# Expert tiles cut into two 64-row halves that stand side by side in TensorE's columns, with a new expert order

## The chip, the cores and the metric

The kernel runs on one core of a Trainium2 chip. The metric is the time of one execution on the device in microseconds (us); three runs were timed, and one further execution was taken by the profiler. The core's engines are TensorE (PE in the profile; its weight loads are listed apart as PEld), VectorE (DVE), ScalarE (ACT), GpSimd (POOL) and SyncE (SP). They run their own instruction lists and meet at semaphores. SP and POOL issue the transfers between device memory and the on-chip memory.

## The reference

The whole program is one step of a decoder layer for 1,024 prompt tokens and 32 sample tokens: a mixer, cross-attention and a mixture of experts, with a LayerNorm after each. Only the mixture of experts is touched. All 1,056 tokens (`TOK`) go through it together; each goes to the two best experts of its best group of four.

```python
N_EXPERTS = 16; N_GROUPS = 4; EXPERTS_PER_GROUP = 4; TOP_K = 2; D_EXPERT = 256; D_MODEL = 1024
...
def moe_ffn(h, w_router, router_bias, wg, wu, wd):
    x = h.reshape(b * t, d)
    s = jax.nn.sigmoid((x @ w_router).astype(jnp.float32))
    sel = (s + router_bias.astype(jnp.float32)).reshape(-1, N_GROUPS, EXPERTS_PER_GROUP)
    group_score = jnp.sum(lax.top_k(sel, TOP_K)[0], axis=-1)
    gidx = jnp.argmax(group_score, axis=-1)
    in_group = jnp.take_along_axis(sel, gidx[:, None, None], axis=1)[:, 0]
    _, local = lax.top_k(in_group, TOP_K)
    eidx = gidx[:, None] * EXPERTS_PER_GROUP + local
    ...
    hg = jnp.einsum('nd,edf->nef', x, wg)
    hu = jnp.einsum('nd,edf->nef', x, wu)
    act = jax.nn.silu(hg) * hu * combine[:, :, None].astype(x.dtype)
    y = jnp.einsum('nef,efd->nd', act, wd)
```

With the reference's inputs the 16 experts get, in order of number, 103, 113, 113, 121, 121, 168, 127, 112, 134, 161, 158, 115, 131, 151, 129 and 155 rows, 2,112 in all. These counts follow from the routing above.

## The kernel before

**Routing.** `stage_route` makes the router's products, ranks the experts of each token, and gives every (token, expert) pair a row in a list that is sorted by expert. Each expert's rows are padded to whole tiles of 128. The program is fixed before the routing is known, so it runs `MOE_TILES` = 32 tiles, the most that any routing needs. With this routing 24 are filled, and the last 8 hold no rows; they are computed all the same, with the weights of the last expert. The results are tables: the expert of each tile (`tile_expert`), the first tile after each expert (`expert_end`), and the token, gate and destination of each row.

**The expert stage.** `stage_experts` walks over the tiles. POOL gathers the 128 token rows of a tile (`gather`), and at the end adds the 128 result rows to device memory (`add_rows`, one at a time). For each tile, PE turns the rows (8 transposes, `turn_x`), multiplies by the gate and up weights (`gate_up`, 8 matmuls over 512 columns, in two parts of four), turns the hidden rows (`turn_hid`, 2 transposes) and multiplies by the down weights (`product_down`, 4 matmuls over 512 columns). In fp32 each of these matmuls is two passes, so two records in the profile. ACT and DVE take the results out of PSUM. The weights are the moving operand, and the token rows the stationary one.

One step of PE for tile t holds the first part of `gate_up(t)`, then `turn_hid(t-1)`, the second part of `gate_up(t)`, `turn_x(t+1)` and `product_down(t-1)`:

```python
                gate_up(j, u, 0, e)
                if not first:
                    turn_hid(*prev)
                gate_up(j, u, 1, e)
                if not last:
                    turn_x(*((j, u + 1) if u < U - 1 else (j + 1, 0)))
                if not first:
                    product_down(*prev, prev_e & 3)
```

ACT's step is `turned_hid(t-1)`, `silu(t)`, `turned_x(t+1)`, `finish(t-1)`; DVE's is `hidden(t)`, `turned_x(t+1)`, `finish(t-1)`. The loop is unrolled by `U` = 4.

**Weights.** An expert has 3 MB of weights, loaded by `load_expert` as three transfers of 1 MB into one of four slots (`c.xw`). The first three experts are loaded during the routing. In the expert stage SP takes the experts in turn: it waits until expert e has landed, tells PE (`w_ok`), waits until the tiles of expert e-2 are done, and issues expert e+2 into the slot that expert e-2 held.

Of the kernel before, what the change touches and what calls it, by code (L numbers as in the profile page):

```python
# [15 lines left out]
I32 = mybir.dt.int32  # L16
# [26 lines left out]
DE = 256  # L43
MOE_TILES = (2 * TOK - NE) // P + NE
ALPHA = float(2 ** 0.25)
# [59 lines left out]


def route_blocks():
# [4 lines left out]
    c = {  # L112
        "tie": row(np.arange(4)[None, :] < np.arange(4)[:, None]),
        "iota128": row(np.arange(P)),
        "iota32": row(np.arange(MOE_TILES)),
        "thr9": row(P * np.arange(9)),
        "tri16": row(np.arange(NE)[None, :] < np.arange(NE)[:, None]),
        "token": np.where(token < TOK, token - TOK, 0),
        "lane": p,
        "valid": token < TOK,  # L120
    }
    return {k: np.asarray(v, np.float32) for k, v in c.items()}
# [39 lines left out]
def setup(nc, ctx, T, O):  # L162
# [87 lines left out]
    c.row_token = ctx.enter_context(nc.sbuf_tensor("row_token", [P, MOE_TILES], I32))  # L250
    c.tile_expert = ctx.enter_context(nc.sbuf_tensor("tile_expert", [1, MOE_TILES], I32))
    c.expert_end = ctx.enter_context(nc.sbuf_tensor("expert_end", [1, NE], I32))
# [2447 lines left out]
def load_expert(c, sp, e):  # L2700

    EW = KC * DE
    for q, name in enumerate(('ex_wg', 'ex_wu', 'ex_wd')):
        sp.dma_start(c.xw[:, e % 4, q * EW:(q + 1) * EW], c.T[name][0, e].rearrange("(p k) f -> p (k f)", p=P))\
            .then_inc(c.xw_in[e % 4], 16)


def stage_route(c):
# [11 lines left out]
            rank=TE, mask=TE, mask0=TE, masked=TE, pre=TE, gs=TILES * G4, grank=TILES * G4, den=TILES,  # L2720
            tiles_cmp=NE * 9, tiles_of=NE, base_cmp=NE * NE, base=NE, ends=NE, exp_cmp=MOE_TILES * NE, exp_f=MOE_TILES,
            rk=2 * TILES, bs=2 * TILES, flo_cmp=2 * TILES * NT, flo=2 * TILES, lo=2 * TILES, hi=2 * TILES,
            slot_f=MOE_TILES, empty=MOE_TILES, one_lo=2 * TILES * P, one_hi=2 * TILES * MOE_TILES,
# [16 lines left out]
    with nc.Block() as block:  # L2740
# [49 lines left out]
        def _(dve):  # L2790
# [55 lines left out]
            for q, m in enumerate((mask0, mask1)):  # L2846
# [18 lines left out]
            ec = c.A("exp_cmp").rearrange("p (s e) -> p s e", e=NE)  # L2865
            link(vt.tensor_tensor(ec, tab("iota32", MOE_TILES).unsqueeze(2).to_broadcast([P, MOE_TILES, NE]),
                                  ends.unsqueeze(1).to_broadcast([P, MOE_TILES, NE]), ALU.is_ge))
            exp_f = c.A("exp_f")
# [3 lines left out]

            link(vt.tensor_scalar(ends, ends, 1.0, None, ALU.add))
            link(vt.tensor_copy(c.expert_end[:], ends[0:1, :]))


            rk, bs, flo, lo, hi = c.A("rk"), c.A("bs"), c.A("flo"), c.A("lo"), c.A("hi")
# [6 lines left out]
            fc = c.A("flo_cmp").rearrange("p (n j) -> p n j", j=NT)  # L2884
            link(vt.tensor_tensor(fc, rk.unsqueeze(2).to_broadcast([P, N2, NT]),
                                  tab("thr9", 9)[:, 1:9].unsqueeze(1).to_broadcast([P, N2, NT]), ALU.is_ge))
            link(vt.tensor_reduce(flo, fc, AX, ALU.add))
            link(vt.scalar_tensor_tensor(lo, flo, -float(P), rk, ALU.mult, ALU.add))
            link(vt.tensor_tensor(hi, bs, flo, ALU.add))
            link(vt.tensor_tensor(one_lo, lo.unsqueeze(2).to_broadcast([P, N2, P]),  # L2890
                                  tab("iota128", P).unsqueeze(1).to_broadcast([P, N2, P]), ALU.is_equal))
            link(vt.tensor_tensor(one_hi, hi.unsqueeze(2).to_broadcast([P, N2, MOE_TILES]),
                                  tab("iota32", MOE_TILES).unsqueeze(1).to_broadcast([P, N2, MOE_TILES]), ALU.is_equal))
            link(vt.tensor_tensor(one_gate, one_hi, c.gate.unsqueeze(2).to_broadcast([P, N2, MOE_TILES]), ALU.mult))
# [18 lines left out]
def stage_experts(c):  # L2913
# [23 lines left out]
    y_ok = [s(f"yok{q}") for q in range(2)]  # L2937
    x_turned, up, sig, hid_ok, hid_turned, hidT_ok, down = (
        s("xturned"), s("up"), s("sig"), s("hid"), s("hturned"), s("hidT"), s("down"))
    U = 4  # L2940
    J = MOE_TILES // U
    XT, UPB, HT, DNB = (0, 1), (2, 3), 4, (6, 7)

    with nc.Block() as block:
        @block.sync
        def _(sp):
            sp.sem_inc(y_ok[1], 1)
            for e in range(NE):
                sp.wait_ge(c.xw_in[e % 4], 48 * (e // 4 + 1))
                sp.sem_inc(w_ok, 1)  # L2950
                if e == 0:
                    load_expert(c, sp, 3)
                if e >= 2 and e + 2 < NE:

# [31 lines left out]
        def _(pe):  # L2986
            def expert(t):
                return pe.value_load(c.tile_expert[0:1, bass.ds(t, 1)], min_val=0, max_val=NE - 1)

            def turn_x(j, u):  # L2990

                t = j * U + u
                pe.wait_ge(x_in[u % 2], 16 * (j * 2 + u // 2 + 1))
                for q in range(2):
                    if not (isinstance(j, int) and t < 1):
                        pe.wait_ge(xT_ok[q], t)
                    for k in range(4):
                        last = nc.tensor.transpose(ps[XT[q]][:, k * P:(k + 1) * P], x[:, u % 2, slice(4 * q + k, D, KC)],
                                                   K("ident"))
                    last.then_inc(x_turned, 1)  # L3000

            def gate_up(j, u, half, e):
                t = j * U + u
                if half == 0:
# [20 lines left out]
            def product_down(j, u, slot):  # L3025
                t = j * U + u
                pe.wait_ge(hidT_ok, t + 1)
                for q in range(2):
                    if not (isinstance(j, int) and t < 1):
                        pe.wait_ge(y_ok[q], t + q)  # L3030
                    for f in range(2):
                        last = nc.tensor.matmul(ps[DNB[q]][:, :], hidT[:, u % 2, f, :], down_of[:, bass.ds(slot, 1), f, q * 512:(q + 1) * 512].rearrange("p a n -> p (a n)"),  # L3032
                                                start=(f == 0), stop=(f == 1))
                    last.then_inc(down, 1)

            def step(j, u, first, last):

                prev = (j, u - 1) if u else (j - 1, U - 1)
                e = expert(j * U + u)
                prev_e = None if first else expert(j * U + u - 1)  # L3040
                gate_up(j, u, 0, e)
# [16 lines left out]
            turn_hid(J - 1, U - 1)  # L3058
            product_down(J - 1, U - 1, expert(MOE_TILES - 1) & 3)

        @block.scalar
        def _(act):
# [15 lines left out]
            def finish(t, u, first):  # L3078

                act.wait_ge(down, 2 * t + 1)  # L3080
                if not first:
# [12 lines left out]

            turned_x(0, 0)
            for u in range(U):
                step(0, u, True, False)
# [9 lines left out]
        def _(dve):  # L3107
# [9 lines left out]
            def finish(t, u, first):  # L3117
                dve.wait_ge(down, 2 * t + 2)
# [4 lines left out]
            def step(j, u, first, last):  # L3123
                hidden(j * U + u, u)
                if not (last and u == U - 1):
# [3 lines left out]

            turned_x(0, 0)  # L3130
            for u in range(U):
                step(0, u, True, False)
# [137 lines left out]
```

## Time and profile before

| what | value |
|---|---|
| median of three runs | 1704.71 us (1702.11 to 1705.04) |
| the profiled execution's time | 1703.08 us |
| its span, first to last instruction | 1701.3 us |
| mean granted TensorE clock | 0.928 of full speed |
| PE busy / DVE busy / ACT busy | 1481.7 / 618.1 / 499.7 us |

The profile's own time is 1.8 us above its span. An engine's busy time is the union of its instructions, and a matmul's end is modelled, so the steps below are read from the starts of instructions. The expert stage runs from about 1258 us to 1657 us of the span, after the routing and before the last LayerNorm.

### The profile page before, as it was taken

To read this page: it belongs to the slowest core of one execution; us is meant where nothing else is said; L and a number is where in the kernel's file an instruction comes from. 1 tells how busy PE (TensorE), PEld (TensorE's weight loads), DVE (VectorE), ACT (ScalarE), POOL (GpSimd) and SP (SyncE) were. 2 spreads that over 40 slices of the span, in tenths; PEclk is the share of its full clock that TensorE was granted. 3 is DMA by queue.
4 is the path that set the end of the run, shared out by engine and by line. 5 is a ranking of instruction groups with operands and counts; after the bars stand their busy time and mean duration, and the time that the engine had idled before them with its cause. 6 is when DMAs were issued, how large, how long until landed. Compare 5 with 4: busy or idle time off the path is not lost. (4 is left out here: it accounts for less than half of the span.)

```text
span 1701.3 us, 24683 instructions
## 1 busy us (share of the span) xinstructions
PE 1481.7 (87%) x9721; PEld 1062.2 (62%) x9722; DVE 618.1 (36%) x1005; ACT 499.7 (29%) x1050; POOL 190.0 (11%) x176
## 2 busy tenths in 40 slices
PE   4998999689999898889979989899459999999950
PEld 2445999545597677768869877687244544544420
DVE  3323462377512234447641033575421111111107
ACT  1124133278614434441222144312001111111114
POOL 0000000023200232200000000000001221222114
PEclk9998999789979799999989999999759999999985
DMA  8110121150013400012141164432625997843435
GB/s 311 56 56 20 44 55 38 36 174 26 1 50 102 136 15 2 3 56 109 44 136 38 50 255 167 147 106 87 247 111 189 329 313 238 252 89 85 97 51 227
DMA packets 85984, 193.37 MB, mean 114 GB/s; under 512 B 13204, under 2 KB 49179, under 8 KB 79475
## 3 DMA queue, kind: packets, MB, share of 16 engines
q1 hardware_dynamic: 76523, 157.14, 25.9%
q0 software_dynamic: 9216, 33.56, 8.5%
q8 instruction: 73, 1.20, 0.3%
q10 hardware_dynamic: 144, 1.25, 0.2%
q14 instruction: 28, 0.23, 0.0%
HBM read 148.50 MB, written 43.51 MB: 113 GB/s over the span
## 5 line engine op out<-in xcount | busy, mean ns | idle before, releaser
L3012 PE MATMUL bank<-arena,hT 128*128 x512 | 233.3, 599 | 2.2 <-DVE hT L3115 2.2
L3012 PEld LDWEIGHTS bank<-arena,hT 128*128 128x128 f32 x512 | 96.1, 193 | 111.3 <-issue 111.3
L3032 PE MATMUL bank<-arena,hT 128*128 x256 | 115.3, 593 | 0.7 <-ACT hT L3070 0.7
L473 PE MATMUL bank<-arena,hT 128*128 128x512 f32 x256 | 112.8, 599 | 0.0
L3110 DVE SCALAR_TENSOR_TENSOR hT<-bank,small,hT 128x256 f32<-128x256 f32 x32 | 15.5, 484 | 224.8 <-ACT hT L3076 224.8
L2134 PE MATMUL bank<-hT_rest,f_w_high 128*128 128x352 f32 x288 | 93.4, 324 | 0.0
L473 PEld LDWEIGHTS bank<-arena,hT 128*128 128x128 f32 x256 | 48.7, 193 | 58.3 <-issue 58.3
L2972 POOL DMA_INDIRECT expert_sums<-hT,row_slot x32 | 50.7, 1586 | 276.4 <-DVE hT L3121 173.0
L3032 PEld LDWEIGHTS bank<-arena,hT 128*128 128x128 f32 x256 | 46.3, 191 | 47.2 <-issue 47.2
L2963 POOL DMA_INDIRECT hT<-tokens,row_token x32 | 31.5, 984 | 317.5 <-POOLq L2740 288.3
L2133 PE MATMUL bank<-hT_high,q_w_high 128*128 128x352 f32 x192 | 62.4, 325 | 4.0 <-DVE q_w_low L2426 4.0
L2133 PE MATMUL bank<-f_h_high_a,f_w_high 128*128 128x352 f32 x180 | 59.0, 328 | 6.7 <-DVE f_w_low L683 6.7
L2135 PE MATMUL bank<-hT_high,q_w_low 128*128 128x352 f32 x192 | 62.9, 328 | 0.0
L2134 PE MATMUL bank<-hT_low,q_w_high 128*128 128x352 f32 x192 | 62.7, 326 | 0.0
L1132 PE MATMUL bank<-arena 128*128 128x256 f32 x256 | 61.7, 401 | 0.3 <-ACT arena L1264 0.3
L2135 PE MATMUL bank<-f_h_high_a,f_w_low 128*128 128x352 f32 x180 | 58.5, 325 | 0.0
L1132 PEld LDWEIGHTS bank<-arena 128*128 128x128 f32 x256 | 51.4, 203 | 9.3 <-issue 0.6
L3070 ACT COPY hT<-bank 128x256 f32<-128x256 f32 x32 | 11.9, 372 | 148.1 <-PE bank L3022 148.1
L2134 PEld LDWEIGHTS bank<-hT_rest,f_w_high 128*128 128x128 f32 x288 | 54.9, 191 | 0.0
L3121 DVE COPY hT<-bank 128x512 f32<-128x512 f32 x32 | 22.1, 691 | 89.6 <-PE bank L3032 86.8
L2133 PE MATMUL bank<-w_w_high,w_s_high 128*128 128x512 f32 x128 | 50.5, 395 | 0.3 <-DVE w_w_low L2320 0.3
L2133 PE MATMUL bank<-o_w_high,o_s_high 128*128 128x512 f32 x128 | 50.5, 395 | 0.0
(470 smaller groups left out, 2963.7 us busy)
## 6 DMA issues: line engine op xcount, KB each, us to landing
arena<-in_ex_wg_dram SPq DMA_DIRECT2D x16, 1024.0 KB, 5.1
arena<-in_ex_wu_dram SPq DMA_DIRECT2D x16, 1024.0 KB, 8.9
arena<-in_ex_wd_dram SPq DMA_DIRECT2D x16, 1024.0 KB, 12.7
tokens<-h SPq DMA_DIRECT2D x24, 512.0 KB, 2.6
arena<-in_cache_mem_k_dram SPq DMA_DIRECT2D x8, 1024.0 KB, 4.9
arena<-in_w_in_dram SPq DMA_DIRECT2D x12, 512.0 KB, 4.1
h<-tokens SPq DMA_DIRECT2D x6, 1024.0 KB, 6.7
h<-in_x_prompt_dram SPq DMA_DIRECT2D x8, 512.0 KB, 8.8
```

The costliest lines, as they stand in the source:

```text
L473: last = nc.tensor.matmul(ps[bank][0:r, 0:n], hT[:, k, i * P:i * P + r], wt[:, k, col:col + n], start=(k == 0), stop=(k == KC - 1))
L1132: last = c.nc.tensor.matmul(c.ps[bank][:, 0:256], c.memT[:, k, m * P:(m + 1) * P], c.mw[:, n % 3, k, :], start=(k == 0), stop=(k == KC - 1))
L2133: nc.tensor.matmul(out, high, w_high, start=start, stop=False)
L2134: nc.tensor.matmul(out, high, w_low, start=False, stop=False)
L2135: return nc.tensor.matmul(out, low, w_high, start=False, stop=stop)
L2963: gp.indirect_dma_start(x[:, t % 2, :], None, c.tokens_dram, bass.IndirectOffsetOnAxis(ap=c.row_token[:, t:t + 1], axis=0)).then_inc(x_in[ ...
L2972: gp.indirect_dma_start(c.sums_dram, bass.IndirectOffsetOnAxis(ap=c.row_slot[:, t:t + 1], axis=0), y[:, t % 2, :], None, compute_op=ALU.ad ...
L3012: last = nc.tensor.matmul(ps[UPB[u % 2]][:, :], xT[:, u % 2, k, :], gate_up_of[:, bass.ds(slot, 1), :, k, :].rearrange("p a g f -> p (a g) ...
L3032: last = nc.tensor.matmul(ps[DNB[q]][:, :], hidT[:, u % 2, f, :], down_of[:, bass.ds(slot, 1), f, q * 512:(q + 1) * 512].rearrange("p a n ...
L3070: nc.scalar.copy(hidT[:, u % 2], ps[HT][:, 0:DE].rearrange("p (f t) -> p f t", f=2)).then_inc(hidT_ok, 1)
L3110: nc.vector.scalar_tensor_tensor(hid[:, u % 2, :], ps[UPB[u % 2]][:, DE:2 * DE], c.row_gate[:, bass.ds(t, 1)], sg[:, u % 2, :], ALU.mult, ...
L3121: nc.vector.tensor_copy(y[:, u % 2, 512:D], ps[DNB[1]][:, :]).then_inc(y_ok[1], 1)
```

## The change

A tile still has 128 rows, but it is now two halves of 64 (`HT_ROWS`), and each half has an expert of its own. Experts are padded to halves of 64, at least one for each expert. The program therefore has at most 48 halves, which make `MOE_TILES` = 24 tiles. With the routing above the halves of the experts in the new order are 2, 2, 3, 3, 2, 3, 3, 3, 2, 2, 3, 3, 2, 2, 2, 3, in all 40: tiles 0 to 19 are filled and 20 to 23 empty.

Each matmul of `gate_up` and `product_down` becomes two, with 64 stationary columns each: the lower half's rows against its expert's slot, written to PSUM partitions 0 to 63, and the upper half's rows against a copy of its expert's weights, written to partitions 64 to 127 of the same bank. The copies alternate between two places (`wb` in the arena, and the free `h`). ACT copies one half of the columns and DVE the other (`copy_gate_up` for tile t+1 and `copy_down` for tile t, both at the front of step t). Experts are taken in the order 0, 4, 8, 12, 1, 5, ... (`ORDER`), so that neighbours are of different groups and no token stands twice in a tile. SP loads expert e (by place in that order) when expert e-4 is done and expert e-1 has landed.

```diff
+HT_ROWS = 64
+HALVES = (2 * TOK - NE) // HT_ROWS + NE
+MOE_TILES = (HALVES + 1) // 2
...
+ORDER = [4 * (j % 4) + j // 4 for j in range(NE)]
...
+            link(vt.tensor_tensor(ec, tab("iota128", H).unsqueeze(2).to_broadcast([P, H, NE]),
+                                  ends.unsqueeze(1).to_broadcast([P, H, NE]), ALU.is_ge))
...
+    c.place(start=4 * 3 * EW, wb=3 * EW)
+    copies = [c.A("wb"), h.rearrange("p i d -> p (i d)")[:, 0:3 * EW]]
...
+    def copy_gate_up(eng, copy, t, u, z, first):
+
+        e = eng.value_load(c.tile_expert[0:1, bass.ds(2 * t + 1, 1)], min_val=0, max_val=NE - 1)
+        eng.wait_ge(w_ok, e + 1)
+        if not first:
+            eng.wait_ge(up, t - 1)
+        copy(whole[u % 2][:, 0:2, z, :], slots[:, bass.ds(e & 3, 1), 0:2, z, :].rearrange("p a q n -> p (a q) n")).then_inc(gu_ok[z], 1)
+
+    def copy_down(eng, copy, t, u, z, first):
+
+        e = eng.value_load(c.tile_expert[0:1, bass.ds(2 * t + 1, 1)], min_val=0, max_val=NE - 1)
+        eng.wait_ge(w_ok, e + 1)
+        if not first:
+            eng.wait_ge(down[1], t - 1)
+        copy(whole[u % 2][:, 2, z, :], slots[:, bass.ds(e & 3, 1), 2, z, :].rearrange("p a n -> p (a n)")).then_inc(dn_ok[z], 1)
...
             sp.sem_inc(y_ok[1], 1)
+            load_expert(c, sp, 3)
             for e in range(NE):
+                if e >= 4:
+                    sp.wait_ge(down[1], sp.value_load(c.expert_end[0:1, ORDER[e - 4]:ORDER[e - 4] + 1], min_val=1, max_val=MOE_TILES))
+                    load_expert(c, sp, e)
                 sp.wait_ge(c.xw_in[e % 4], 48 * (e // 4 + 1))
                 sp.sem_inc(w_ok, 1)
-                if e == 0:
-                    load_expert(c, sp, 3)
-                if e >= 2 and e + 2 < NE:
-
-                    sp.wait_ge(y_ok[1], sp.value_load(c.expert_end[0:1, e - 2:e - 1], min_val=1, max_val=MOE_TILES + 1))
-                    load_expert(c, sp, e + 2)
...
+                if half == 0:
+                    for q in range(2):
+                        pe.wait_ge(gu_ok[q], t + 1)
                 slot = e & 3
                 for k in range(4 * half, 4 * half + 4):
-                    last = nc.tensor.matmul(ps[UPB[u % 2]][:, :], xT[:, u % 2, k, :], gate_up_of[:, bass.ds(slot, 1), :, k, :].rearrange("p a g f -> p (a g) f"), start=(k == 0), stop=(k == KC - 1))
+                    nc.tensor.matmul(ps[UPB[u % 2]][rows_of(0), :], xT[:, u % 2, k, rows_of(0)],
+                                     gate_up_of[:, bass.ds(slot, 1), :, k, :].rearrange("p a g f -> p (a g) f"),
+                                     start=(k == 0), stop=(k == KC - 1))
+                    last = nc.tensor.matmul(ps[UPB[u % 2]][rows_of(1), :], xT[:, u % 2, k, rows_of(1)], gate_up_b[u % 2][:, :, k, :],
+                                            start=(k == 0), stop=(k == KC - 1))
...
                 for q in range(2):
+                    pe.wait_ge(dn_ok[q], t + 1)
...
                 if not (first and u == 0):
                     turned_hid(j * U + u - 1, (u - 1) % U)
+                if not (last and u == U - 1):
+                    copy_gate_up(act, nc.scalar.copy, t + 1, u + 1, 0, first and u == 0)
+                copy_down(act, nc.scalar.copy, t, u, 0, first and u < 2)
                 silu(t, u, first and u < 2)
...
             turned_x(0, 0)
+            copy_gate_up(act, nc.scalar.copy, 0, 0, 0, True)
...
+                if not (last and u == U - 1):
+                    copy_gate_up(dve, nc.vector.tensor_copy, t + 1, u + 1, 1, first and u == 0)
+                copy_down(dve, nc.vector.tensor_copy, t, u, 1, first and u < 2)
                 hidden(j * U + u, u)
```

In PE's list, one part of `gate_up` and `turn_hid` stood as follows in the first, unrolled steps before (ISA rows set the address of the slot, 128x512 is partitions by columns of the output):

```order
L3012 ISA
L3012 MATMUL bank<-arena,hT 128x512
L3012 ISA
L3012 MATMUL bank<-arena,hT 128x512
L3012 ISA
L3012 MATMUL bank<-arena,hT 128x512
L3022 MATMUL bank<-const,hT 128x128 x2
```

In the changed kernel the same place reads as follows (L3048 is the lower half, L3051 the upper one from the copy, L3062 `turn_hid`):

```order
L3048 ISA
L3048 MATMUL bank<-arena,hT 64x512
L3051 MATMUL bank<-arena,hT 64x512
L3048 ISA
L3048 MATMUL bank<-arena,hT 64x512
L3051 MATMUL bank<-arena,hT 64x512
L3062 MATMUL bank<-const,hT 128x128 x2
```

Each 128-row matmul has become a pair of 64-row matmuls that follow each other directly; the transposes are as they were, so a step goes from the 64-row form to the 128-row form and back twice.

On ACT, a step in the tile loop before held these rows (hidden copy, silu, x copy, result copy):

```order
L3070 COPY hT<-bank 128x256
L3073 REGISTER_ALU
L3076 ACTIVATE hT<-bank 128x256
L3065 ISA
L3066 COPY hT<-bank 128x512
L3080 ISA
L3082 REGISTER_ALU
L3083 COPY hT<-bank 128x512
```

Now two loads of the tile's expert number and two copies stand between the hidden copy and the silu (from the gate and up copy, L2965, on; L2973 is the down copy, L3121 the silu, L3111 the x copy, L3128 the result copy):

```order
L2965 COPY arena<-arena 128x2x1024
L2969 TENSOR_LOAD tile_expert
L2969 ISA x2
L2970 REGISTER_ALU
L2973 REGISTER_ALU
L2973 ISA
L2973 COPY h<-arena 128x1024
L3121 ACTIVATE hT<-bank 128x256
L3111 COPY hT<-bank 128x512
L3127 REGISTER_ALU
L3128 COPY hT<-bank 128x512
```

The silu of tile t and everything behind it on ACT now come after the copy for tile t+1, and so after the wait for that tile's weights.

## Rows read from the trace of the kernel before

**Rows 1.** The page: span, and busy time of PE and the others.
```profile
span 1701.3 us, 24683 instructions
PE 1481.7 (87%) x9721; PEld 1062.2 (62%) x9722; DVE 618.1 (36%) x1005; ACT 499.7 (29%) x1050; POOL 190.0 (11%) x176
```
**Rows 2.** Timeline of one tile's step: start, us, engine, line, instructions merged.
```profile
1614.93 3.60 PE L3012 MATMUL bank<-arena,hT 128*128 x8
...
1618.37 0.39 PE L3022 MATMUL bank<-const,hT 128*128 128x128 f32 x2
...
1618.80 0.37 ACT L3070 COPY hT<-bank 128x256 f32<-128x256 f32 x1 [4.79 <-PE bank L3022]
1622.03 1.05 PE L2998 MATMUL bank<-const,hT 128*128 128x128 f32 x8
1622.23 0.38 ACT L3076 ACTIVATE hT<-bank 128x256 f32<-128x256 f32 x1 [3.06 <-PE bank L3012]
1622.65 0.48 DVE L3110 SCALAR_TENSOR_TENSOR hT<-bank,small,hT 128x256 f32<-128x256 f32 x1 [6.82 <-ACT hT L3076]
1622.67 0.58 ACT L3066 COPY hT<-bank 128x512 f32<-128x512 f32 x1
1622.92 3.60 PE L3032 MATMUL bank<-arena,hT 128*128 x8
1623.12 0.69 DVE L3115 COPY hT<-bank 128x512 f32<-128x512 f32 x1
...
1626.35 3.60 PE L3012 MATMUL bank<-arena,hT 128*128 x8
```
**Rows 3.** Two steps: length, busy time by engine, granted clock, DMA share, GB/s.
```profile
1306.60:1318.00 11.40, 11.40 (x35) 5.69 (x34) 1.86 (x3) 1.93 (x4) 2.58 (x2) 1.00 1.02 373
...
1489.30:1500.70 11.40, 11.40 (x35) 5.69 (x34) 1.77 (x3) 1.93 (x4) 2.57 (x2) 1.00 0.43 92
```
**Rows 4.** PE's timeline, column tiles of 32 (L464) in the first stage.
```profile
144.40 3.66 PE L464 MATMUL bank<-arena,hT 128*32 128x256 f32 x64
147.99 0.44 PE L483 MATMUL bank<-const,arena 128*128 128x128 f32 x2
```
**Rows 5.** Group by line: 256 columns, full array, one after the other.
```profile
L2537 PE MATMUL bank<-arena 128*128 128x256 f32 x128 | 30.6, 394 | 0.8 <-PEq L2393 0.8
```
**Rows 6.** PE's timeline, column tiles of 64 (L1009) behind a full-array matmul.
```profile
400.19 0.59 PE L994 MATMUL bank<-arena,const 128*128 128x512 f32 x1
400.71 0.66 PE L1009 MATMUL bank<-arena 128*64 128x128 f32 x8
```
**Rows 7.** The weight loads of the same place, and all of that line.
```profile
400.71 0.41 PEld L1009 LDWEIGHTS bank<-arena 128*64 128x64 f32 x8 [0.76 <-issue]
...
L1009 PEld LDWEIGHTS bank<-arena x288: 132/137/138, 356.4 to 458.6; 128*64 128x64 f32 x144
```
**Rows 8.** PE's timeline, from column tiles to full-array transposes.
```profile
986.72 0.83 PE L2526 MATMUL bank<-arena 128*32 128x256 f32 x12
987.48 1.09 PE L2548 MATMUL bank<-const,arena 128*128 128x128 f32 x8
```
**Rows 9.** Weight loads: first issues of two experts in a row, landing time.
```profile
1341.87 0.33 SPq L2704 DMA_DIRECT2D arena<-in_ex_wg_dram  x1
...
1364.71 0.33 SPq L2704 DMA_DIRECT2D arena<-in_ex_wg_dram  x1
...
arena<-in_ex_wd_dram SPq DMA_DIRECT2D x16, 1024.0 KB, 12.7
```
**Rows 10.** Nearest rows for the copies and the loads of a number.
```profile
L640 ACT ACTIVATE arena<-arena 128x2304 f32<-128x2304 f32 x1 | 2.1, 2135 | 0.0
...
L712 DVE TENSOR_SCALAR h<-arena,h 128x1024 f32<-128x1024 f32 x6 | 4.5, 745 | 0.0
...
L2988 PEldq TENSOR_LOAD <-tile_expert x64: 296/303/935, 1268.5 to 1634.6; - x64
```
**Rows 11.** Start of the expert stage.
```profile
1270.47 0.69 DVE L3115 COPY hT<-bank 128x512 f32<-128x512 f32 x1 [12.64 <-PE bank L2998]
...
1271.51 10.16 PE L3012 MATMUL bank<-arena,hT 128*128 x16 [1.08 <-DVE hT L3115]
```
**Rows 12.** PE idle and what follows: columns as in rows 3, clock third from the end.
```profile
859.20:865.90 6.70, 0.01 (x1) 0.00 (x0) 5.89 (x9) 1.46 (x4) 0.00 (x0) 0.65 1.12 309
865.90:874.90 9.00, 4.96 (x18) 4.60 (x19) 5.38 (x6) 4.11 (x5) 0.00 (x0) 0.50 0.64 229
```
**Rows 13.** One of the routing's DVE operations, by size.
```profile
L2866 DVE TENSOR_TENSOR arena<-arena 128x512 f32<-128x512 f32 x1 | 0.7, 694 | 0.0
```

More of the change, by code:

```diff
@@ L114, in route_blocks @@
         "iota128": row(np.arange(P)),
-        "iota32": row(np.arange(MOE_TILES)),
-        "thr9": row(P * np.arange(9)),
-        "tri16": row(np.arange(NE)[None, :] < np.arange(NE)[:, None]),
+        "half_start": row(np.concatenate([[-1], HT_ROWS * np.arange(1, MAXH)])),
+        "tile_start": row(P * np.arange(1, MOE_TILES)),
+        "tri16": row(np.argsort(ORDER)[None, :] < np.argsort(ORDER)[:, None]),
         "token": np.where(token < TOK, token - TOK, 0),
@@ L2937, in stage_experts @@
     y_ok = [s(f"yok{q}") for q in range(2)]
-    x_turned, up, sig, hid_ok, hid_turned, hidT_ok, down = (
-        s("xturned"), s("up"), s("sig"), s("hid"), s("hturned"), s("hidT"), s("down"))
+    x_turned, up, sig, hid_ok, hid_turned, hidT_ok = (
+        s("xturned"), s("up"), s("sig"), s("hid"), s("hturned"), s("hidT"))
     U = 4
     J = MOE_TILES // U
+    gu_ok, dn_ok = [s(f"gu{q}") for q in range(2)], [s(f"dn{q}") for q in range(2)]
+    down = [s(f"down{q}") for q in range(2)]
+    c.place(start=4 * 3 * EW, wb=3 * EW)
+    copies = [c.A("wb"), h.rearrange("p i d -> p (i d)")[:, 0:3 * EW]]
+    gate_up_b = [x[:, 0:2 * EW].rearrange("p (g k f) -> p g k f", g=2, k=KC) for x in copies]
+    down_b = [x[:, 2 * EW:].rearrange("p (j n) -> p j n", j=2) for x in copies]
+    whole = [x.rearrange("p (q z n) -> p q z n", q=3, z=2) for x in copies]
+    slots = c.xw.rearrange("p s (q z n) -> p s q z n", q=3, z=2)
+    def copy_gate_up(eng, copy, t, u, z, first):
[10 more added lines that the diff above has]
+        copy(whole[u % 2][:, 2, z, :], slots[:, bass.ds(e & 3, 1), 2, z, :].rearrange("p a n -> p (a n)")).then_inc(dn_ok[z], 1)
     XT, UPB, HT, DNB = (0, 1), (2, 3), 4, (6, 7)
@@ L2988, in expert, with rows_of @@
                 return pe.value_load(c.tile_expert[0:1, bass.ds(t, 1)], min_val=0, max_val=NE - 1)
+            def rows_of(half):
+                return slice(half * HT_ROWS, (half + 1) * HT_ROWS)
             def turn_x(j, u):
@@ L3028, in product_down @@
                 for q in range(2):
+                    pe.wait_ge(dn_ok[q], t + 1)
+                for q in range(2):
                     if not (isinstance(j, int) and t < 1):
@@ L3031, in product_down @@
                     for f in range(2):
-                        last = nc.tensor.matmul(ps[DNB[q]][:, :], hidT[:, u % 2, f, :], down_of[:, bass.ds(slot, 1), f, q * 512:(q + 1) * 512].rearrange("p a n -> p (a n)"),
-                                                start=(f == 0), stop=(f == 1))
-                    last.then_inc(down, 1)
+                        nc.tensor.matmul(ps[DNB[q]][rows_of(0), :], hidT[:, u % 2, f, rows_of(0)],
+                                         down_of[:, bass.ds(slot, 1), f, q * 512:(q + 1) * 512].rearrange("p a n -> p (a n)"),
+                                         start=(f == 0), stop=(f == 1))
+                        last = nc.tensor.matmul(ps[DNB[q]][rows_of(1), :], hidT[:, u % 2, f, rows_of(1)],
+                                                down_b[u % 2][:, f, q * 512:(q + 1) * 512], start=(f == 0), stop=(f == 1))
+                    last.then_inc(down[q], 1)
             def step(j, u, first, last):
                 prev = (j, u - 1) if u else (j - 1, U - 1)
-                e = expert(j * U + u)
-                prev_e = None if first else expert(j * U + u - 1)
+                e = expert(2 * (j * U + u))
+                prev_e = None if first else expert(2 * (j * U + u - 1))
                 gate_up(j, u, 0, e)
@@ L3058, in _ @@
             turn_hid(J - 1, U - 1)
-            product_down(J - 1, U - 1, expert(MOE_TILES - 1) & 3)
+            product_down(J - 1, U - 1, expert(2 * (MOE_TILES - 1)) & 3)
         @block.scalar
@@ L3078, in finish @@
             def finish(t, u, first):
-                act.wait_ge(down, 2 * t + 1)
+                act.wait_ge(down[0], t + 1)
                 if not first:
@@ L3117, in finish @@
             def finish(t, u, first):
-                dve.wait_ge(down, 2 * t + 2)
+                dve.wait_ge(down[1], t + 1)
                 if not first:
@@ L3130, in _ @@
             turned_x(0, 0)
+            copy_gate_up(dve, nc.vector.tensor_copy, 0, 0, 1, True)
             for u in range(U):
```

39 lines of the change are left out of this document (20 added, 19 removed).

## The prediction

> **What bounds the kernel now.** I read the page first: PE is busy 87% of the span [rows 1]. The question is then whether the expert stage is one of the stretches that PE fills. The timeline of one step says so. Four matmuls of `gate_up` start at 1614.93, the hidden transposes at 1618.37, the x transposes at 1622.03, the down matmuls at 1622.92, and the next tile's `gate_up` at 1626.35, with no idle time noted on any PE row [rows 2]. A step is 1626.35 - 1614.93 = 11.42 us; eight passes take 1618.37 - 1614.93 = 3.44 us, so a pass of 512 columns takes 0.43 us. The windows of two steps show PE busy for all of the time at the full clock, ACT and DVE for under 2 us each [rows 3]. Transfers are not the limit on the average: a step with an expert's load has a DMA share of 1.02 at 373 GB/s, one without 0.43 at 92 GB/s [rows 3], and PE runs alike in both. So the stage costs 32 steps of 11.42 us, and the 8 empty tiles cost as much as the filled ones.
>
> **What the change removes.** Eight steps of 11.42 us are -91.4 us [rows 2]. This holds if a pair of 64-row matmuls takes as long as one of 128 rows did.
>
> **Does a pair run side by side?** Before has no pair with 512 moving columns, but it has others. In the first stage 64 passes of 256 columns, four column tiles of 32 side by side, take 147.99 - 144.40 = 3.59 us, or 0.056 us each [rows 4]; one after the other on the full array such a pass takes 30.6 / 128 = 0.239 us [rows 5]. That is four at a time. With tiles of 64, eight passes of 128 columns are done 0.66 us after their start, modelled end included [rows 6]; the full array's eight transposes of the same width take 1.05 us [rows 2]. I take 0.43 us for a pair, as for one pass. Each further 0.01 us for a pair would cost 24 tiles x 24 pairs x 0.01 = 5.8 us.
>
> The weight loads decide the same question. The eight loads of L1009 all happen within 0.41 us from 400.71, although each takes 137 ns, so they overlap with each other and with the passes that run from 400.71 to 401.37 [rows 6, 7]. The Trainium skill (TensorE: Matmul & The Clock Gate, "Part 3: Packing small matmuls — row/col tiling") says that a weight load overlaps a running matmul only where the row groups differ, and both halves here use all rows. By that rule each pair would wait for a load, and the change would lose; that case is the third rival below, and by the rows I take the load as hidden.
>
> **Added on PE: changes of form.** From the full array to 64 columns: the last full matmul starts at 400.19 and needs 0.43, the next starts at 400.71, so 0.09 us are lost [rows 6]. Back to the full array: three groups of four 256-column passes, at 4 x 0.056 = 0.22 us each, run from 986.72 to about 987.38, the transposes start at 987.48, which is 0.10 us later, and their eight take 1.09 us where they took 1.05 [rows 2, 8]; together 0.15 us. A step has two of each kind, 0.5 us, so a step becomes 11.92 us, and 24 steps cost +12.0 us more. If the second pass's load is exposed too after each change to 64 columns (the pair of L1009 loses some 0.05 us there), it is 2.4 us more; no gain is possible here.
>
> **Added on ACT and DVE: copies.** ACT copies 2,048 and 1,024 columns per tile. The nearest row is 2,135 ns for 2,304 columns [rows 10]; at that rate 1.9 and 1.0 us. DVE: 745 ns for 1,024 columns [rows 10], so about 1.4 and 0.7 us; if it ran at the rate of an operation with two inputs, 694 ns for 512 [rows 13], 2.8 and 1.4. Each copy needs the tile's expert number: on PE such a load takes 303 ns, at worst 935 [rows 10]; with the register rows around it I take 0.65 us, and 1.1 as the bound. What they hide behind is PE's step. ACT begins its hidden copy 1618.80 - 1614.93 = 3.9 us into the step [rows 2], ends it at 4.4 with a change of form ahead, the two copies with their numbers at 8.7, the silu 0.38 us later at 9.1; DVE's hidden product (0.48) ends at 9.6 and its x copy (0.69) at 10.3 [rows 2]. PE needs xT at 11.9, so 1.6 us are spare, and the copies cost nothing. At 1.1 us for each number still 0.7 is spare. Beyond a growth of 1.6 us on ACT every microsecond would cost 24. DVE's copies come earlier, from the step's start on, and have more room. PE's waits for `gu_ok` and `dn_ok` are then met before they are reached.
>
> At the start nothing hides them. `gate_up(0)` starts at 1271.51, right behind DVE's x copy, which ends at 1270.47 + 0.69 = 1271.16 [rows 11]. Now 0.65 + 1.4 us come in between: +2 us (+3.5 at DVE's slower rate). The 16 passes run at half clock for their first part there, as before (10.16 us for 16 [rows 11]).
>
> **Routing.** The table comparisons grow from 144 to 272, from 512 to 768 and from 144 to 414 columns, two operations each; four others shrink by 144, 144, 72 and 72. At the slope that 694 ns for 512 gives with some 0.16 us of it fixed, about 1.04 ns per column, this is (1308 - 432) x 1.04 = +0.9 us, all of it on a chain in which each operation waits for the one ahead.
>
> **Weights.** Before, two loads could be under way; now the next one is issued only when the last has landed. A load takes 12.7 us to its last landing beside gathers and result rows [rows 9], a step 11.9. The slot of the expert at place j comes free when the tiles of j-4 are done, and a tile is done one step after its own. In the trace of before that pace is seen in the issues, one step (11.42 us) after a one-tile expert and two (1364.71 - 1341.87 = 22.84) after a two-tile one [rows 9]. I went through all places with the 40 halves. Most loads land a step or more before use. Those of places 9, 10, 13 and 14 land 0.1 to 0.3 steps into the step in which the copy for their first tile runs, which ACT, starting 4.4 us into it, does not notice. One is late: place 15 begins in the upper half of tile 18, and waits for place 11, which ends in tile 15, done as step 17 begins. The load lands 12.8 us later, 0.9 after the end of step 17. Meanwhile ACT stands at `copy_gate_up(18)` with `silu(17)` behind it. After the landing come the copies, silu and x copy on ACT, the hidden product and x copy on DVE: 1.9 + 0.65 + 1.0 + 0.38 + 0.48 + 0.69 = 5.1 us, handoffs 0.2. PE idles 0.9 + 5.3 = 6.2 us. After an idle time of 6.70 us before, the granted clock was 0.50 throughout the next 9.00 us, which held another idle time [rows 12]; I take 6 us of work at the lower level, 1.2 GHz, which loses 3. Together +9.3 us (0 if the load lands 7 us sooner).
>
> **Sum**, against the profiled execution's 1703.1 us (1.6 below the median): -91.4 + 12.0 + 2 + 0.9 + 9.3 = -67.2, so 1635.9; I say 1636, and 1624 to 1650 for this case (no late weights, or the exposed loads and two more late tiles).
>
> **Rivals.**
> 1. *Weights late at several tiles.* If a load takes 16 us instead of 12.7, which a DMA share of 1.02 with one load speaks for and the 12.7 of the row against [rows 3, 9], places 12 to 15 follow each other at 16 us where a tile takes 11.9, and tiles 12, 16, 17 and 18 wait, by estimate 2.5, 3.6, 4.2 and 5.5 us. That is 9.6 us more than above, and three more stretches at half clock, 9 us: 1655.
> 2. *Pairs out of step by one pass.* In fp32 a matmul is two passes. Taken strictly in list order, the upper half's first pass would run with the lower half's second, and each of three groups of matmuls in a step would take one pass more, 3 x 0.43 = 1.3 us, 31 us in all: 1667. Rows 4 to 6 speak against it, but there no address is set between two matmuls.
> 3. *Weight loads exposed (slower).* Where every pair must wait for a load of 137 ns [rows 7], a step takes 24 x 0.137 = 3.3 us more, 79 us in all: 1715. It decides from 67 / 576 = 0.117 us per pair on. That is the skill's rule of row groups; the overlapping loads of L1009 contradict it.
> 4. *No overlap (slower).* With the halves one after the other each pair takes 0.43 us more: 576 x 0.43 = 248 us, 1884. The rows of two other stages contradict it; dynamic addresses and 512 columns are what they lack.
>
> **How the numbers follow.** The forecast has 0.72, rival 1 0.10, rival 2 0.05, rival 3 0.03, rival 4 0.04; that the late load is not late or the changes of form are hidden (1614 to 1624) 0.05; no effect 0.01. A measurement here tells from no change what is over 0.2%. Faster: 0.72 + 0.10 + 0.05 + 0.05 = 0.92; same 0.01; slower 0.07. The range 1616 to 1672 holds the forecast, rival 1, rival 2 and most of the better case.
>
> **What would show it.** Right: 24 steps, about 11.9 us from one `gate_up` to the next; pairs of 64-row passes starting together every 0.43 us; PE idle some 6 us once, at tile 18, ended by DVE's x copy, with the clock at 0.50 behind it; `gate_up(0)` about 2 us later than 1271.5. Wrong: steps over 12.5 us; PE waiting at `gu_ok` or xT in ordinary steps; idle times at other tiles; pairs spaced by more than 0.43 us.

## The result and the profile after

The changed kernel takes 1639.56 us (median of 4 runs, 1637.99 to 1644.93) where the kernel before took 1704.0 beside it: a ratio of 0.9626 [0.9602, 0.9649], inside the predicted range and 3.6 us from the forecast. The rows below are from one execution of 1640.94 us.

The page, in the form of [rows 1]:
```profile
span 1638.9 us, 25689 instructions
...
PE 1413.3 (86%) x10025; PEld 993.3 (61%) x10026; DVE 649.2 (40%) x1030; ACT 550.2 (34%) x1067; POOL 179.4 (11%) x160
...
L3048 PE MATMUL bank<-arena,hT 128*64 x384 | 176.9, 605 | 9.3 <-DVE hT L3164 5.4
```
PE is busy 68.4 us less, DVE and ACT 31 and 50 us more: they have the copies. Of PE's 9.3 us of idle time at `gate_up`, 5.4 are one wait on DVE's x copy.

The timeline in the form of [rows 2], at three places: the start of the stage, one ordinary step, and tile 18. L3048 and L3051 are the lower and upper half of `gate_up`, L3062 `turn_hid`, L3031 `turn_x`, L3074 `product_down`, L2965 and L2973 the copies of weights.
```profile
1278.34 1.23 DVE L2965 COPY arena<-arena 128x2048 f32 x1 [0.51 <-issue]
...
1279.92 1.11 PE L3048 MATMUL bank<-arena,hT 128*64 x1 [2.82 <-DVE arena L2965]
...
1400.27 0.59 PE L3048 MATMUL bank<-arena,hT 128*64 x1
1400.27 0.14 PEld L3048 LDWEIGHTS bank<-arena,hT 128*64 128x64 f32 x1 [0.29 <-issue]
1400.28 0.59 PE L3051 MATMUL bank<-arena,hT 128*64 128x512 f32 x1
1400.28 0.14 PEld L3051 LDWEIGHTS bank<-arena,hT 128*64 128x64 f32 x1
...
1400.70 0.59 PE L3048 MATMUL bank<-arena,hT 128*64 x1
...
1403.28 0.59 PE L3048 MATMUL bank<-arena,hT 128*64 x1
...
1403.81 0.51 PE L3062 MATMUL bank<-const,hT 128*128 128x128 f32 x2
1404.24 0.64 PE L3048 MATMUL bank<-arena,hT 128*64 x1
...
1404.72 0.59 PE L3048 MATMUL bank<-arena,hT 128*64 x1
...
1405.29 1.90 ACT L2965 COPY h<-arena 128x2048 f32 x1 [0.56 <-issue]
...
1407.09 1.04 ACT L2973 COPY arena<-arena 128x1024 f32 x1
...
1412.40 0.59 PE L3048 MATMUL bank<-arena,hT 128*64 x1
...
1485.37 0.33 SPq L2710 DMA_DIRECT2D arena<-in_ex_wg_dram  x1
...
1498.16 1.90 ACT L2965 COPY arena<-arena 128x2048 f32 x1 [8.55 <-SPq L2986]
1498.19 1.23 DVE L2965 COPY arena<-arena 128x2048 f32 x1 [12.03 <-SPq L2986]
...
1499.96 1.04 ACT L2973 COPY h<-arena 128x1024 f32 x1
1500.91 0.37 ACT L3121 ACTIVATE hT<-bank 128x256 f32<-128x256 f32 x1
...
1501.83 0.68 DVE L3164 COPY hT<-bank 128x512 f32<-128x512 f32 x1
...
1502.82 1.11 PE L3048 MATMUL bank<-arena,hT 128*64 x1 [5.36 <-DVE hT L3164]
```
Read it in this order. The two halves start together (1400.27 and 1400.28) and the next pair starts 0.43 us later, as one 128-row pass did [rows 2]. The step from 1400.27 to 1412.40 is 12.13 us, where [rows 2] have 11.42. The extra time is at the changes of form: the transposes start 1403.81 - 1403.28 = 0.53 us after the last pair, the two of them take 1404.24 - 1403.81 = 0.43 us (0.22 in the run with 128-row matmuls below), and the first pair behind them takes 1404.72 - 1404.24 = 0.48 us. ACT's copies take 1.90 and 1.04 us in the middle of PE's work, and no PE row there notes idle time. At tile 18 both copying engines wait for SP, 8.55 and 12.03 us, and PE then waits for what stands behind those copies.

Windows, with the columns of [rows 3], for two ordinary steps, the idle time at tile 18, and the two steps behind it:
```profile
1400.27:1412.40 12.13, 12.13 (x61) 4.55 (x59) 3.67 (x5) 4.67 (x6) 3.34 (x2) 1.00 0.92 312
1412.40:1424.53 12.13, 12.13 (x61) 4.56 (x59) 3.68 (x5) 4.67 (x6) 3.33 (x2) 1.00 0.61 163
...
1497.30:1502.82 5.52, 0.16 (x3) 0.01 (x1) 3.22 (x5) 4.09 (x5) 0.00 (x0) 0.94 0.21 85
1502.82:1516.32 13.50, 13.50 (x58) 4.94 (x60) 3.18 (x5) 4.67 (x6) 2.81 (x2) 0.90 0.36 78
1516.32:1528.45 12.13, 12.13 (x60) 4.55 (x58) 3.60 (x5) 4.66 (x6) 3.33 (x2) 1.00 0.42 86
```
The step behind the idle time takes 1.37 us longer at a mean clock of 0.90. The starts of its first four pairs are 0.85 to 0.91 us apart instead of 0.43.

The transfers issued from 1485 to 1500, with the size and the time from issue to landing:
```profile
arena<-in_ex_wg_dram SPq DMA_DIRECT2D x1, 1024.0 KB, 4.7
arena<-in_ex_wu_dram SPq DMA_DIRECT2D x1, 1024.0 KB, 7.4
arena<-in_ex_wd_dram SPq DMA_DIRECT2D x1, 1024.0 KB, 11.7
```
The down weights, issued at 1486.22, land at 1497.9, 0.6 us after step 17 would have given way to step 18.

**Where the time went.** From its first weight load (1258.47 before, 1265.26 after) to the last `turn_hid` (1636.88 and 1575.82) the stage takes 378.41 us before and 310.56 after: -67.85. The rest of the span's -62.4 us is +0.97 from the routing, -1.3 behind the stage, and +5.8 ahead of the routing, where the change touches nothing.

### The profile page after: what moved, and what is told of

Read it like the earlier page. It is cut to its first block and busy times, and to the rows that moved or that the text cites. A ratio compares the mean times of both kernels' runs of the same rounds, so it can differ in the third digit from the quotient of the medians.

```text
span 1638.9 us, 25689 instructions
## 1 busy us (share of the span) xinstructions
PE 1413.3 (86%) x10025; PEld 993.3 (61%) x10026; DVE 649.2 (40%) x1030; ACT 550.2 (34%) x1067; POOL 179.4 (11%) x160
## 3 DMA queue, kind: packets, MB, share of 16 engines
q8 instruction: 75, 1.23, 0.3%
## 5 line engine op out<-in xcount | busy, mean ns | idle before, releaser
L3048 PE MATMUL bank<-arena,hT 128*64 x384 | 176.9, 605 | 9.3 <-DVE hT L3164 5.4
L3048 PEld LDWEIGHTS bank<-arena,hT 128*64 128x64 f32 x384 | 51.2, 139 | 110.7 <-issue 107.9
L3051 PE MATMUL bank<-arena,hT 128*64 128x512 f32 x192 | 90.0, 614 | 0.0
L3074 PE MATMUL bank<-arena,hT 128*64 x192 | 87.5, 598 | 0.7 <-ACT hT L3115 0.7
L3051 PE MATMUL bank<-h,hT 128*64 128x512 f32 x192 | 87.0, 595 | 0.0
L479 PEld LDWEIGHTS bank<-arena,hT 128*128 128x128 f32 x256 | 48.6, 192 | 58.1 <-issue 58.0
L3002 POOL DMA_INDIRECT expert_sums<-hT,row_slot x24 | 47.4, 1976 | 220.9 <-DVE hT L3170 177.8
L2993 POOL DMA_INDIRECT hT<-tokens,row_token x24 | 24.2, 1010 | 317.0 <-POOLq L2746 289.7
L3159 DVE SCALAR_TENSOR_TENSOR hT<-bank,small,hT 128x256 f32<-128x256 f32 x24 | 11.6, 484 | 115.7 <-ACT hT L3121 115.7
L3074 PEld LDWEIGHTS bank<-arena,hT 128*64 128x64 f32 x192 | 24.4, 136 | 45.2 <-issue 42.5
```

What stands on the lines that cost most here:

```text
L479: last = nc.tensor.matmul(ps[bank][0:r, 0:n], hT[:, k, i * P:i * P + r], wt[:, k, col:col + n], start=(k == 0), stop=(k == KC - 1))
L2993: gp.indirect_dma_start(x[:, t % 2, :], None, c.tokens_dram, bass.IndirectOffsetOnAxis(ap=c.row_token[:, t:t + 1], axis=0)).then_inc(x_in[ ...
L3002: gp.indirect_dma_start(c.sums_dram, bass.IndirectOffsetOnAxis(ap=c.row_slot[:, t:t + 1], axis=0), y[:, t % 2, :], None, compute_op=ALU.ad ...
L3048: nc.tensor.matmul(ps[UPB[u % 2]][rows_of(0), :], xT[:, u % 2, k, rows_of(0)], gate_up_of[:, bass.ds(slot, 1), :, k, :].rearrange("p a g f ...
L3051: last = nc.tensor.matmul(ps[UPB[u % 2]][rows_of(1), :], xT[:, u % 2, k, rows_of(1)], gate_up_b[u % 2][:, :, k, :], start=(k == 0), stop=( ...
L3074: nc.tensor.matmul(ps[DNB[q]][rows_of(0), :], hidT[:, u % 2, f, rows_of(0)], down_of[:, bass.ds(slot, 1), f, q * 512:(q + 1) * 512].rearra ...
```

## The experiments

The kernel before ran beside each group: 1704.97 us (7 runs) beside the first four, 1703.78 (9 runs) beside the last three. Single runs of one kernel spread by up to 9 us, and the medians of the lower halves alone, the small copies and the transposes together lie inside the 1637.99 to 1644.95 us of the changed kernel's own runs or about 1 us below. So what these three edits do is read from the steps in the traces and not from the whole time. The new order of experts was not run by itself; what it alone does to the time is open.

**The lower halves alone.** The upper half's matmuls are left out, the copies stay.
```diff
-  nc.tensor.matmul(ps[UPB[u % 2]][rows_of(0), :], ...)
-  last = nc.tensor.matmul(ps[UPB[u % 2]][rows_of(1), :], ... gate_up_b[u % 2][:, :, k, :] ...)
+  last = nc.tensor.matmul(ps[UPB[u % 2]][rows_of(0), :], ...)
```


> Leaves out the upper half's matmuls (rows 64 to 127 of each product are not computed); loads, copies and waits stay. Theory (a pair takes what one pass takes, the 0.71 us by which a step grew are four changes of form): passes still every 0.43 us, the step stays at 12.13 us, the time within 3 us of the changed kernel's 1639.6. Rival (running two halves costs TensorE something in each pair): the step falls towards 11.4 us and the time by up to 16 us, to about 1624.

Measured: 1637.23 us (1635.58 to 1644.14), ratio 0.9618 [0.9587, 0.9648], an ordinary step of 12.11 us against 12.13 with both halves. Taking half of the matmuls away gives 0.02 us per step, so the upper half costs next to nothing and the 0.7 us of growth are not its price. PE's timeline of one step (here L3060 is `turn_hid`, L3072 `product_down`):
```profile
1399.71 0.50 PE L3060 MATMUL bank<-const,hT 128*128 128x128 f32 x2
1400.14 3.65 PE L3048 MATMUL bank<-arena,hT 128*64 x8
1403.72 1.16 PE L3031 MATMUL bank<-const,hT 128*128 128x128 f32 x8
1404.81 3.65 PE L3072 MATMUL bank<-arena,hT 128*64 x8
1408.30 3.60 PE L3048 MATMUL bank<-arena,hT 128*64 x8
1411.83 0.51 PE L3060 MATMUL bank<-const,hT 128*128 128x128 f32 x2
```

**All 128 rows in one matmul.** Everything else is as in the change, the copies too, but the upper half is computed with the lower half's expert.
```diff
-  nc.tensor.matmul(ps[UPB[u % 2]][rows_of(0), :], xT[:, u % 2, k, rows_of(0)], ...)
-  last = nc.tensor.matmul(ps[UPB[u % 2]][rows_of(1), :], ...)
+  last = nc.tensor.matmul(ps[UPB[u % 2]][:, :], xT[:, u % 2, k, :], ...)
```


> Each pair is replaced by one 128-row matmul against the lower half's expert (the upper half's rows meet the wrong weights); copies and waits for them stay. Theory: no change of form is left, the step is 11.42 us as before, the time falls by 23 x 0.71 = 16 us to about 1623. Rival (the copies, or the waits for them, set the step of 12.13 us): the step stays near 12.1 us and the time near 1640.

Measured: 1624.89 us (1621.82 to 1628.09), ratio 0.9531 [0.9507, 0.9555]; the step is 11.42 us again. The same piece of a step on PE:
```profile
1409.06 0.39 PE L3060 MATMUL bank<-const,hT 128*128 128x128 f32 x2
1409.28 3.60 PE L3048 MATMUL bank<-arena,hT 128*128 x8
1412.72 1.05 PE L3031 MATMUL bank<-const,hT 128*128 128x128 f32 x8
1413.61 3.60 PE L3072 MATMUL bank<-arena,hT 128*128 x8
1417.04 3.60 PE L3048 MATMUL bank<-arena,hT 128*128 x8
1420.47 0.39 PE L3060 MATMUL bank<-const,hT 128*128 128x128 f32 x2
```
From start to start the five pieces take 0.22, 3.44, 0.89, 3.43 and 3.43 us here, and 0.43, 3.58, 1.09, 3.49 and 3.53 in the run above: +0.21, +0.14, +0.20, +0.06 and +0.10, together 0.71. So the whole growth of a step lies at the four changes of form: each piece that borders on one has a part of it. This run takes away both the changes and the 64-column form; the run with the transposes together, below, takes away changes alone. With the shorter step the loads are late a little earlier too (steps 15 and 16 take 11.82 and 11.61), and the idle time at tile 18 is 6.27 us.

**Small copies.** From the third tile on only an eighth of the weights is copied, so the upper halves use wrong weights there.
```diff
+  n = 1024 if first else 128
-  copy(whole[u % 2][:, 0:2, z, :], slots[:, bass.ds(e & 3, 1), 0:2, z, :]...)
+  copy(whole[u % 2][:, 0:2, z, 0:n], slots[:, bass.ds(e & 3, 1), 0:2, z, 0:n]...)
```


> From the third tile on only one eighth of each weight copy is made (the rest of the copy is stale). Theory (copies are hidden behind PE except behind the late load): ordinary steps stay at 12.13 us, the idle time at tile 18 is shorter by about 2.5 us, the time falls by 2 to 4 us. Rival (the copies slow PE in every step, by their reads or by holding up ACT): the step falls below 12.0 us and the time by 6 us or more.

Measured: 1636.94 us (1634.54 to 1641.6), ratio 0.9603 [0.9582, 0.9624]; the step stays 12.13 us. The copies are hidden in ordinary steps. At tile 18 PE idles 4.01 us instead of 5.36: 1.4 us shorter, where 2.5 was expected. ACT's two copies become 2.2 us shorter in sum (0.41 and 0.30 us), but DVE's x copy, which releases PE, comes at 1502.30, behind ACT's second copy, which waits 0.44 us for its expert number.
```profile
1503.32 0.64 PE L3050 MATMUL bank<-arena,hT 128*64 x1 [4.01 <-DVE hT L3166]
```

**The transposes together.** PE makes all of `gate_up` and then both groups of transposes, so that a step has two changes of form. For ACT the hidden copy then stands behind the copies of weights.
```diff
   gate_up(j, u, 0, e)
+  gate_up(j, u, 1, e)
   if not first:
       turn_hid(*prev)
-  gate_up(j, u, 1, e)
...
-  if not (first and u == 0):
-      turned_hid(j * U + u - 1, (u - 1) % U)
   ... copy_gate_up(act, ...); copy_down(act, ...)
+  if not (first and u == 0):
+      turned_hid(j * U + u - 1, (u - 1) % U)
```


> The hidden transposes move behind both parts of gate_up, next to the x transposes, and ACT's hidden copy behind the weight copies; the result is the same. Theory (what costs is each change between the 64-row and the 128-row form): two of four changes go, the step falls by half of 0.71 to 11.77 us, the time by about 8 us to 1631. Rival (the hidden copy is now late for product_down, or the 0.71 us are a cost of the pairs): the step is 12.1 us or longer, the time 1640 or more.

Measured: 1638.08 us (1633.55 to 1642.34), ratio 0.962 [0.959, 0.965]. The step is 11.78 us: half of the 0.71 is gone, with all pairs still there, so it is the changes that cost. The time is hardly better, since steps 15 to 17 take 12.82, 12.64 and 22.07 us:
```profile
1490.99 1.90 ACT L2965 COPY arena<-arena 128x2048 f32 x1 [14.09 <-SPq L2986]
...
1493.74 0.36 ACT L3115 COPY hT<-bank 128x256 f32<-128x256 f32 x1
...
1494.38 1.11 PE L3074 MATMUL bank<-arena,hT 128*64 x1 [8.27 <-ACT hT L3115]
```
The same late load now holds up the hidden copy (L3115) as well, and PE stops at `product_down(16)`, ahead of work that it could do before. It idles 8.27 us instead of 5.36, and the clock is at 0.50 for 10.2 us. From its first weight load to the last `turn_hid` the stage takes 308.96 us, 1.6 us less than in the changed kernel (3.5 less than in its repeat, below), where 8 were expected. The theory was right on the step, and the rival on the late hidden copy that takes most of the gain.

**The changed kernel once more**, for the comparisons below; nothing is edited.


> The changed kernel as it is, to see how far its time and the stretch ahead of the experts move from one execution to the next. Theory (the 6 us by which the routing began later in its profile are a matter of the execution, from half-clock stretches in the delta stage): the same time within 0.3%, and the routing's first weight load starts at another time than 1202 us of the span, nearer to the 1196 of before. Rival (the change moved the stages ahead of the experts): it starts at 1202 again.

Measured: 1643.63 us (1640.08 to 1644.95), ratio 0.9637 [0.9612, 0.9663]; the step is 12.13, and steps 17 and 18 take 17.82 and 15.08 us: the stall costs 8.6 us here, since the clock was at 0.50 for 6.8 us instead of 3.4:
```profile
1505.66 1.11 PE L3048 MATMUL bank<-arena,hT 128*64 x1 [5.52 <-DVE hT L3164]
...
1505.66:1520.74 15.08, 15.08 (x59) 5.30 (x61) 3.16 (x5) 4.67 (x6) 2.81 (x2) 0.81 0.32 70
```
The routing's first weight load starts at 1203.91, so the expected lower value did not come here. In the eight profiled kernels with the change or an edit of it, which are alike up to that point, it starts from 1197.02 to 1203.91 (1195.65 before). So executions of one code spread by 6.9 us there; the one value of before lies 1.4 us below the lowest of the eight. The values fall into two groups, and one stretch far ahead of the routing tells them apart. Here it is in the changed kernel and in the last run below, whose code is the same up to there:
```profile
608.00:629.00 21.00, 19.91 (x233) 15.16 (x234) 4.81 (x11) 3.09 (x9) 7.67 (x9) 0.52 0.08 17
...
608.00:629.00 21.00, 19.13 (x367) 15.79 (x367) 7.35 (x16) 5.23 (x16) 8.42 (x9) 0.92 0.13 28
```
The five profiles with a mean granted clock of 0.51 to 0.56 there (the changed kernel in both executions, the 128-row matmuls, the small copies, the split load) begin the routing at 1201.47 us or later; the three with 0.92 begin it at 1197.02 to 1197.68, and before, also with 0.92, at 1195.65. So most of the +5.8 us belongs to the execution and not to the change, as the theory had it. Why the clock differs there from one execution to the next is open.

**The load in two parts.** The gate and up weights are issued when `gate_up` of the old expert's last tile is done, the down weights when its `product_down` is, and each copy waits for its own part.
```diff
-  sp.wait_ge(down[1], ...expert_end...)
-  load_expert(c, sp, e)
-  sp.wait_ge(c.xw_in[e % 4], 48 * (e // 4 + 1))
+  sp.wait_ge(up, end)
+  load_expert(c, sp, e, (0, 1))
+  sp.wait_ge(down[1], end)
+  load_expert(c, sp, e, (2,))
+  sp.wait_ge(c.xw_in[e % 4], 32 * (e // 4 + 1))
   sp.sem_inc(w_ok, 1)
+  sp.wait_ge(c.xd_in[e % 4], 16 * (e // 4 + 1))
+  sp.sem_inc(wd_ok, 1)
```


> The gate and up weights of an expert are loaded as soon as gate_up of the last tile in their slot is done, the down weights when its product_down is done, with a semaphore of their own; the result is the same. Theory (the idle time at tile 18 comes from the load that waits for its slot and blocks ACT): that idle time goes, with the half-clock stretch behind it, and the time falls by 6 to 7 us to about 1633. Rival (the loads are limited by the transfers themselves, or the down weights come late instead): an idle time of several us is left at tile 17 to 19 and the time falls by less than 3 us.

Measured: 1633.15 us (1630.88 to 1635.75), ratio 0.9581 [0.9555, 0.9607]. All steps from the third on take 12.12 or 12.13 us, the clock does not fall between `gate_up(1)` and the last tile, and the stage takes 303.73 us, 6.8 and 8.7 less than in the two runs of the change as it is, whose stalls cost 6.9 and 8.6. SP's issues at that place:
```profile
1471.20 0.33 SPq L2713 DMA_DIRECT2D arena<-in_ex_wg_dram  x1
1471.57 0.43 SPq L2713 DMA_DIRECT2D arena<-in_ex_wu_dram  x1
1486.54 0.33 SPq L2713 DMA_DIRECT2D arena<-in_ex_wd_dram  x1
```
The first two megabytes go out 15 us ahead of the third and are there before the copy needs them. So the stall at tile 18 was the late load: nothing of it is left. Step 17, as a window:
```profile
1486.33:1498.46 12.13, 12.13 (x60) 4.55 (x58) 3.60 (x5) 4.77 (x6) 3.33 (x2) 1.00 0.63 173
```

**All together.** The two edits above, and at the start of the stage the first copies of weights ahead of the first x copy on ACT and DVE.
```diff
-  turned_x(0, 0)
   copy_gate_up(act, nc.scalar.copy, 0, 0, 0, True)
+  turned_x(0, 0)
```


> The turns side by side, the split loads, and the copy for tile 0 made before its rows are there; the result is the same. Theory: the three gains add, 8 us of form changes, 6.9 us of the late load and 1.9 us at the start, 17 us in all: about 1623, 4.8% below before. Rival (what one saves another takes, for instance the hidden copy on ACT behind a blocked weight copy): a gain of under 10 us, about 1630 or more.

Measured: 1621.93 us (5 runs, 1618.96 to 1627.33), ratio 0.9527 [0.9501, 0.9554]; it is faster than both kernels. Two of its steps, as windows, and its first `gate_up`, from the timeline:
```profile
1398.30:1410.08 11.78, 11.78 (x62) 4.57 (x59) 3.60 (x5) 4.57 (x6) 3.33 (x2) 1.00 0.86 270
1410.08:1421.86 11.78, 11.78 (x62) 4.57 (x59) 3.70 (x5) 4.57 (x6) 2.61 (x2) 1.00 0.70 193
```
```profile
1274.23 1.11 PE L3056 MATMUL bank<-arena,hT 128*64 x1 [1.15 <-issue]
```
With the loads in time the gain of the transposes together is there: 22 steps of 0.35 us less are 7.7 us, and the stage (296.12 us) is 7.6 shorter than with the split load alone. Of the 1.9 us expected at the start 0.7 came: `gate_up(0)` starts 1.4 us sooner behind the stage's first weight load, but step 0 is 0.7 us longer, as the clock rose 5.2 us after it began and not 3.7. A new wait of 0.66 us at `product_down(22)`, right behind its transposes, takes those 0.7 back. PE's idle time ahead of `gate_up(0)` falls from 2.82 to 1.15 us.

## Why the prediction was right, step by step

**Eight steps less, and a pair as long as one pass: right.** The pairs stand 0.43 us apart, and the run with the lower halves alone shows that the upper one is free. The third and fourth rival (weight loads exposed, no overlap) fall with that, and the second too: the two halves of a pair start within 0.01 us of each other, although the slot's address is set between one matmul of the lower half and the next.

A load of 64 columns takes 139 ns in `gate_up` and 136 in `product_down` by the page's groups, as in [rows 7]. A pair brings two of them and is no longer than a pass with its one load was, so they are hidden: the two loads of 0.14 us at 1400.27 and 1400.28 stand beside a running pair and end long before the next one at 1400.70. By the rule of the Trainium skill (TensorE: Matmul & The Clock Gate, "Part 3: Packing small matmuls — row/col tiling") these loads would not overlap, since both halves use all rows. The runs of this case contradict it for halves of the columns. So does the kernel before for the full array, where all loads use all rows: the loads of `gate_up` took 0.19 us each, beside passes that followed each other every 0.43 us. That trace already spoke against the third rival.

**Changes of form: right in kind, mis-sized.** This is the term that was off: 0.50 us per step were predicted, 0.71 measured, so that a step is 12.13 and not 11.92 us. One round trip was put at 0.09 us into the 64-column form and 0.15 back. It is 0.10 us ahead of the transposes, 0.11 between the first and the second transpose, 0.10 ahead of the next pair, and 0.05 between the first two pairs: 0.36. The pair's 0.05 was named, but left out of the sum; the second transpose was taken from [rows 8], where it lost some 0.04 us behind column tiles of 32. Over the stage this term and the one transpose group of the last tile come to 16.0 us instead of 12.0. The Trainium skill (TensorEngine Tiling (Array Packing), "Key Properties") says that a change of the tiling mode drains TensorE; the two gaps of 0.10 us agree with that, and the 0.16 us behind them is measured here in addition. Why the second instruction behind a change is late was not tested.

**Copies: right.** They are hidden in ordinary steps, with 1.90 and 1.04 us on ACT (predicted 1.9 and 1.0) and 1.23 and 0.69 on DVE (1.4 and 0.7). The loads of the expert number were put at 0.65 us each on ACT; the first shows as 0.56 us of idle time, and the second not at all (the second copy starts 1407.09 - 1405.29 = 1.80 us after the first one, which takes 1.90).

**The start: close.** `gate_up(0)` stands 14.66 us behind the stage's first weight load, before 13.04: +1.6, predicted +2. What was not foreseen is that step 0 is then 1.0 us shorter (11.16 against 12.14), as the clock rose 3.8 us after `gate_up(0)` began and not 6.1 as before.

**Routing: right.** From its first weight load to that of the stage it is 63.79 us, before 62.82: +0.97, predicted +0.9.

**The late load: at the predicted tile, a little smaller.** It was to land 12.8 us after step 17 began and cost 6.2 us of idle time and 3 of clock, 9.3 in all. It landed 12.8 us after (1497.94 - 1485.16); step 17 ended 0.2 us later than assumed, since steps are longer, and the chain behind the landing took 4.9 us instead of 5.3: the second number, put at 0.65, cost nothing here either (1498.16 to 1499.96), while the handoffs took more than the 0.2 allowed. The lengths of steps 17 and 18 sum it up: 17.66 + 13.51 - 2 x 12.13 = 6.9 us. PE waited for weights at no other tile, so the first rival falls. But it was near, and ACT did notice the two loads ahead, which the prediction had ruled out: they landed 4.8 and 6.2 us into steps 15 and 16, 0.4 and 0.5 of a step instead of 0.1 to 0.3, and ACT was idle for 1.24 and 1.97 us ahead of those copies instead of 0.56. The spare time in the step took that up; with steps of 11.42 or 11.78 us the two steps ahead of it began to wait as well.

**The sum.** For the stage -91.4 + 12.0 + 2 + 9.3 = -68.1 was predicted and -67.85 came, as -91.4 + 16.0 + 0.6 (start and step 0) + 6.9. So the total was met in part by luck, as two errors of size cancelled: +4 at the changes of form, -3.8 at the start and the stall. The profiled execution is 4.9 us above the forecast because of the 5.8 us ahead of the routing, most of which belongs to the execution; the median is 3.6 above.

## What to carry to other kernels

Two 64-row tiles side by side took as long as one 128-row tile, but here each switch between that form and the full array cost about 0.18 us, so put the full-array work of a step together. Before doing so, look at what the moved instruction then stands behind on the other engines: a copy that waits for a load, placed ahead of a hand-off that PE needs, makes one late load cost more. Where a slot is freed in parts, wait and load in parts: 15 us of earlier issue for two thirds of the data removed the only stall.

## What the runs showed that was not expected

After nearly the same idle time the clock came back at different times: idle for 5.36 us, the granted clock was 0.50 (1.2 GHz) for 3.4 us in one execution; idle for 5.52 us, for 6.8 us in another of the same kernel. One stall thus cost 6.9 and 8.6 us. And the same three-megabyte load takes 11.7 us to its last landing when issued at once, while its last megabyte issued by itself, in the run with the load in two parts, takes 4.7 us at that place (issued at 1486.54, when the other two had landed). By this comparison more than half of the 11.7 us is time behind the two transfers issued ahead of it.
